# A transformer block kernel: the memory's norm and scaling moved into the linear attention's stage

## The chip, the cores and the metric

The kernel runs on one core of one Trainium2 chip. The metric is the device time of one execution in microseconds (us). In profiles PE is TensorE, DVE VectorE (Vector), ACT ScalarE (Scalar), POOL GpSimd (Pool) and SP SyncE, whose queue issues the loads.

## What is computed

Two blocks of two layers each, on a sequence of 512 tokens and 1024 features, all in float32. The change lies in both layers of the second block:

```
for i in range(2):
    hn = rmsnorm(h, ln_mix[i]);  aq, ak, av, hy, gq, gk, gv, go, glr, gates = split(hn @ w_in[i])
    y_a = attention(aq, ak, av) @ w_br_attn[i]          # branch 0
    y_b = hyena(hy) @ w_br_hyena[i]                     # branch 1
    y_c = gated_linear_attention(gq, gk, gv, go, glr) @ w_br_gla[i]   # branch 2
    h = h + (g0 * y_a + g1 * y_b + g2 * y_c) @ w_out[i]
    mn = rmsnorm(mem, ln_mem[i])                        # mem: 256 x 1024, the same in both layers
    h = h + cross_attention(rmsnorm(h, ln_x[i]), k = rmsnorm(mn @ wk), v = mn @ wv)
    h = h + square(relu(rmsnorm(h, ln_mlp[i]) @ w1)) @ w2
```

## The kernel before

Activations lie transposed in SBUF: 128 partitions of features by 512 tokens, column block by column block. Every large product is made from halves: a tensor is split into a rounded high half, which Scalar writes, and the remainder, which Vector writes (`rest`), and `mm3` sums three matmuls, high by high, high by low and low by high (lines 841 to 843). Weights come through three raw tiles (WRAW) and three split tiles (WSP): SP loads one, Scalar rounds it (line 1177), Pool subtracts (line 1518), TensorE multiplies. A projection of 1024 features takes 24 matmuls of 512 tokens, a branch's output block takes 12, and one of the memory's key projections (xk) 24 of 256 columns.

`order_of_work` writes the program as a list of steps (Unit). Where several chains run beside each other, `merged` picks the next step: the first chain in the order of its arguments whose step is due, by the times in `pe_time` and the distances in `needs`. A step that is not yet due yields to another chain. Each of the five engines' programs walks the same list and issues its own part of each step, in order. So a step that waits on one engine holds all later steps on that engine.

Each layer's `mix_second` ends with two merged stages. In the first, the linear attention (`main`: lr, gfront, gscan, gvtok, gk, gq, gexp, gmul, gturn, gstate, ginside, grun, and for each of four heads go, gout, gss, gbc, gy, split YC) is merged with the gates and output blocks of branch 0, which read the tile YAB. In the second, `memory` is merged with `last`: eight output blocks of branch 2 ("by", 12 matmuls each), the merge of the gated branches into M (products on lines 1924 and 1927, then `split` M: high half on line 1262, low half on line 1750), and the output projection (wo). The last branch's blocks take merge banks in turn:

```
return (S0, S1)[c % 2] if ab == "a" else (S0, S1, O)[c % 3]
...
b = take_pj(u) if u.pj else take(merge_bank(u.a[0], u.a[3]), dve_done, ("lo", "M", u.a[0:2], u.a[3]))
```

so a block waits until the M that used its bank has its low half. Steps with `pj` use three other banks in rotation, each free when its reader on Scalar or Vector is done.

The memory's steps are: mld (four loads into MT), msq (four squares on Scalar, line 1446, three additions on Vector, line 2159), mnorm (sum over partitions on TensorE, lines 1118 and 1119; root on Scalar, line 1449; reciprocal on Vector, line 2163), msplit (two scalings per tile on Vector, line 2170; high half on Scalar, line 1454; low half by `rest`, line 1624), then xk and xkss for four heads and eight xv. gld loads the parked gates of branch 2 (MBG). Tiles share the SBUF arena by position: MN (the split memory) lies at 8 to 15, where YAB is, and MACC and KSQ at 44 to 46, where the linear attention has QD and AM.

Of the kernel before, what the change touches and what calls it, by code (L numbers as in the profile page):

```python
# [118 lines left out]
def needs(u):  # L119

    k, a = u.kind, u.a
# [6 lines left out]
    if k == "idx":  # L128
        l, c, i = a
# [3 lines left out]
    if k == "sel":  # L133
        l, i, r = a
# [13 lines left out]
    if k == "sc":  # L148
        ab, l, c, i = a
# [42 lines left out]
    if k == "gbc":  # L192
        return [(("gss", *a), 1.8)]
    if k == "mnorm":
        return [(("msq", a[0]), 5.0)]
    if k == "msplit":
        return [(("mnorm", a[0]), 2.8 + 1.6 * a[1])]
    if k == "xkss":
        return [(("xk", *a, 1), 1.8)]
    if k == "xk":  # L200
        return [(("msplit", a[0], 3), 2.6)]
    if k == "xq":
        return [(("xsc", a[0], a[1] - 2), 0.0)]
    if k == "xqss":
# [48 lines left out]
    if k == "vturn":  # L253
        return [(("vs", a[0]), 1.2)]
    if k == "msq":
        return [(("mld", a[0]), 3.0)]
    if k == "split" and a[0] in ("YA", "YC") and a[1][0] == "a":
        return [(("cb" if a[0] == "YA" else "pmix", a[1][1], a[2]), 2.0)]
    if k == "split" and a[0] == "M" and a[1][0] == "b":
# [42 lines left out]
def order_of_work(steps):  # L302
# [100 lines left out]
    def mix_second(l):  # L403
# [58 lines left out]
        for hp in range(2):  # L462
# [8 lines left out]
            for hh in range(2):  # L471
                main += [proj("go", l, hp, hh, src=H, w=[(*B, "go", 2 * hp + hh)]), Unit("gout", l, hp, hh, o=True),
                         Unit("gss", l, hp, hh, pj=True), Unit("gbc", l, hp, hh, pj=True), Unit("gy", l, hp, hh), Unit("split", "YC", B, 2 * hp + hh)]
        out += merged(main, gated("b", l, x, 0, ("YA", B), False, False))
        last = [Unit("gld", l)]
        for c in range(8):
            last.append(proj("by", "b", l, 2, c, False, True, src=("YC", B), w=[(*B, "br", 2, c)]))
# [2 lines left out]
        last += [Unit("split", "M", B, 7)] + out_product(x, "wo", l, "b", ("M", B))  # L480
        return out + merged(memory(l), last)

    def memory(l):
        B = ("b", l)
        out = [Unit("mld", l), Unit("msq", l), Unit("mnorm", l, pj=True)] + [Unit("msplit", l, j) for j in range(4)]
        for hd in range(4):
            out += [Unit("xk", l, hd, kk, src=("MN", l), w=[(*B, "xk", 2 * hd + kk)], pj=True) for kk in range(2)]
            out += [Unit("xkss", l, hd, pj=True)]
        for half in range(2):
            out += [Unit("xv", l, half, j, src=("MN", l), w=[(*B, "xv", half, j)], t=(j == 0)) for j in range(4)]  # L490
        return out
# [77 lines left out]
def program(nc, ins, place, out, steps=8):  # L569
    ctx = ExitStack()  # L570
    with ctx:
# [40 lines left out]
        GS = at(53, "GS", 4)  # L612

        MN, MT, KM, VM = at(8, "MN", 8, fp32r), at(57, "MT", 4), at(49, "KM", 4), at(53, "VM", 4)
        MACC, KSQ = at(46, "MACC", 1), at(44, "KSQ", 2)
        YX, XQ, XSQ, XP, XPT = at(8, "YX", 16, fp32r), at(24, "XQ", 4), at(28, "XSQ", 4), at(32, "XP", 8), at(40, "XPT", 4)

        YM, XN, MR = at(0, "YM", 32, fp32r), at(32, "XN", 8), at(40, "MR", 4)

        XLS = {0: PA, 1: PA, 2: at(40, "XLB", 4), 3: at(60, "XLC", 4)}  # L620
        SQA, SQB, SQC, SQD = at(49, "SQA", 2), at(62, "SQB", 2), at(44, "SQC", 2), at(47, "SQD", 2)

        fixed("ARENA", [128, ARENA, 512])
# [542 lines left out]
        def scalar(e):  # L1166
# [32 lines left out]
            for u in plan:  # L1199
# [222 lines left out]
                elif k == "gturn":  # L1422
                    l, hp = a
                    w.wait_ge(mm_done, ("gturn", l, hp, 0))
                    e.activation(ES[:, 2 * hp, :], banks[T0][:, :], ACT.Copy).then_inc(*act_done.up(("kd", l, hp, 0)))
                elif k == "gout":
                    l, hp, hh = a
                    if hp:
                        w.wait_ge(dve_done, ("lo", "YC", ("b", l), hh))
                    w.wait_ge(mm_done, (k, *a))  # L1430
                    e.activation(GS[:, hh, :], banks[O][:, :], ACT.Square).then_inc(*act_done.up(("gsq", *a)))
                elif k == "gss":
                    l, hp, hh = a
                    w.wait_ge(mm_done, (k, *a))
                    if hp:
                        w.wait_ge(mm_done, ("gbc", l, 0, hh))
                    e.activation(SM[:, 11, 4 * hh:4 * hh + 4], pj(u)[:, 0:4], ACT.Sqrt, scale=1.0 / 128, bias=eps).then_inc(
                        *act_done.up(("pj", u.pj), (k, *a)))
                elif k == "msq":
                    l = a[0]  # L1440
                    for j in range(4):
                        w.wait_ge(landed, ("mem", l, j))
                        o = MACC[:, 0, :] if j == 0 else KSQ[:, j % 2, :]
                        if j == 3:
                            w.wait_ge(dve_done, ("macc", l, 1))
                        e.activation(o, MT[:, j, :], ACT.Square).then_inc(*act_done.up(("msq", l, j)))
                elif k == "mnorm":
                    w.wait_ge(mm_done, (k, *a))
                    e.activation(MACC[:, 0, 0:256], pj(u)[:, 0:256], ACT.Sqrt, scale=1.0 / DM, bias=eps).then_inc(
                        *act_done.up(("pj", u.pj), (k, *a)))  # L1450
                elif k == "msplit":
                    l, j = a
                    w.wait_ge(dve_done, ("mn", l, j))
                    e.activation(halves(MN, j)[0], MT[:, j, :], ACT.Copy).then_inc(*act_done.up(("mhi", l, j)))
                elif k == "xk":
                    l, hd, kk = a
                    if hd:
                        w.wait_ge(mm_done, ("xkss", l, hd - 1))
                    else:
                        w.wait_ge(dve_done, ("macc", l, 3))  # L1460
                    w.wait_ge(mm_done, (k, *a))
                    square_and_copy(u, KSQ[:, kk, 0:256], KM[:, hd, 256 * kk:256 * kk + 256], par(f"xkn{l}", kk), 256,
                                    ("xksq", *a), ("xk", *a))
                elif k == "xkss":
                    l, hd = a
                    if hd:
                        w.wait_ge(dve_done, ("xkm", l, hd - 1, 1))
                    w.wait_ge(mm_done, (k, *a))
                    e.activation(MACC[:, 0, 256:512], pj(u)[:, 0:256], ACT.Sqrt, scale=1.0 / 256, bias=eps).then_inc(
                        *act_done.up(("pj", u.pj), (k, *a)))  # L1470
                elif k == "xv" and a[2] == 3:
                    l, half, j = a
                    w.wait_ge(mm_done, (k, *a))
                    for i, b in enumerate((T0, T1)):
                        e.activation(VM[:, 2 * i + half, :], banks[b][:, :], ACT.Copy).then_inc(*act_done.up(("xvout", l, half, i)))
                elif k == "xq":
                    l, hd, kk = a
                    if hd > 1:
                        w.wait_ge(mm_done, ("xsc", l, hd - 2, 1))
                    w.wait_ge(dve_done, ("scaled", u.pj))  # L1480
                    square_and_copy(u, XSQ[:, 2 * (hd % 2) + kk, :], XQ[:, 2 * (hd % 2) + kk, :], par(f"xqn{l}", kk), 512,
                                    ("xqsq", *a), ("xq", *a))
                elif k == "xqss":
                    l, hd = a
                    w.wait_ge(mm_done, (k, *a))
                    if hd > 1:
                        w.wait_ge(act_done, ("xexp", l, hd - 2, 3))
                    e.activation(SM[:, 14 + hd % 2, 0:4], pj(u)[:, 0:4], ACT.Sqrt, scale=1.0 / 256, bias=eps).then_inc(
                        *act_done.up(("pj", u.pj), (k, *a)))
                elif k == "xsc":  # L1490
                    l, hd = a
                    m = SM[:, 6 + hd % 2, :]
                    w.wait_ge(dve_done, ("xneg", l, hd))
                    if hd > 1:
                        w.wait_ge(mm_done, ("xtr", l, hd - 2, 1))
                    for i in range(4):
                        e.activation(XP[:, 4 * (hd % 2) + i, 0:256], banks[(S0, S1)[i // 2]][:, 256 * (i % 2):256 * (i % 2) + 256],
                                     ACT.Exp, bias=m[:, 4 + i:5 + i], scale=SM[:, 14 + hd % 2, i:i + 1],
                                     accum_out=m[:, 8 + i:9 + i]).then_inc(*act_done.up(("xexp", l, hd, i)))
                elif k == "xtr":  # L1500
                    l, hd = a
                    if hd > 1:
                        w.wait_ge(mm_done, ("xpv", l, hd - 2, 1))
                    w.wait_ge(mm_done, ("xtr", l, hd, 1))
                    e.activation(XPT[:, 2 * (hd % 2) + 1, :], banks[T1][:, :], ACT.Copy).then_inc(*act_done.up(("xpt", l, hd, 1)))
# [105 lines left out]
        def vector(e):  # L1611
# [75 lines left out]
            for u in plan:  # L1687
# [472 lines left out]
                elif k == "mnorm":  # L2160
# [1 line left out]
                    w.wait_ge(act_done, (k, *a))  # L2162
                    e.reciprocal(MACC[:, 0, 0:256], MACC[:, 0, 0:256]).then_inc(*dve_done.up(("mrs", l)))
                    w.wait_ge(dve_done, ("mrs", l))
                elif k == "msplit":
                    l, j = a
                    w.wait_ge(act_done, ("msq", l, 3))
                    for kk in range(2):
                        x = MT[:, j, 256 * kk:256 * kk + 256]
                        e.scalar_tensor_tensor(x, x, par(f"lnm{l}", 2 * j + kk), MACC[:, 0, 0:256], ALU.mult, ALU.mult).then_inc(  # L2170
                            *dve_done.up(("mn0" if kk == 0 else "mn", l, j)))
                    w.wait_ge(act_done, ("mhi", l, j))
                    w.wait_ge(dve_done, ("mn", l, j))
                    rest(*halves(MN, j), MT[:, j, :], ("mlo", l, j))
# [465 lines left out]
```

## Time and profile before

| what | value |
|---|---|
| median of three runs | 3678.8 us (3678.72 to 3684.36) |
| profiled execution | 3681.5 us |
| its span in the profile | 3679.5 us |
| TensorE busy | 3482.4 us |
| Vector, Scalar, Pool busy | 1624.3, 1372.9, 1742.1 us |
| mean granted TensorE clock | 0.967 |

The span runs from the first to the last instruction in the profile. Busy time sums an engine's instructions. The granted clock is the share of full speed (2.4 GHz) that TensorE was given; 0.50 is 1.2 GHz. Matmuls overlap, so the distance between two starts, not the printed duration, is what one costs.

### The profile page before, as it was taken

The numbers are of one execution on the slowest core, as the hardware profiler recorded it, in microseconds if no ns is written. First come the engines' busy times: TensorE is split into PE (matmuls) and PEld (weight loads), VectorE is DVE, ScalarE is ACT, GpSimd is POOL, SyncE is SP. The second block draws the span as 40 slices with busy tenths as digits, with TensorE's granted clock in tenths as the row PEclk, the third lists the DMA queues.
The fourth block names the chain that finished last, engine by engine and source line by source line (L and its number), as shares of the span: only waits on it lengthen the run. The fifth ranks groups of instructions, "written<-read, shape, count | busy, mean of one in ns | idle before, by whom it ended". The sixth has DMA issues, their size and how long they took to land.

```text
span 3679.5 us, 41406 instructions
## 1 busy us (share of the span) xinstructions
PE 3482.4 (95%) x15784; PEld 2747.3 (75%) x15784; DVE 1624.3 (44%) x2605; ACT 1372.9 (37%) x2076; POOL 1742.1 (47%) x1336
## 2 busy tenths in 40 slices
PE   8999999999999987999998999999798999999999
PEld 6778787778777676668786788877675787768887
DVE  5365434366436885434432321268744434223120
ACT  3333543332543334434344322233344434443221
POOL 4454245444244774234362555657632434526564
PEclk9999999999999999989899999999899999999999
DMA  4322224223224322212351333332321214424332
GB/s 155 104 73 85 75 92 151 93 89 93 71 78 147 109 95 89 67 55 69 100 172 58 126 111 97 119 105 95 106 67 58 68 56 149 141 66 141 98 97 92
DMA packets 128846, 359.56 MB, mean 98 GB/s; under 512 B 16766, under 2 KB 17086, under 8 KB 128648
## 3 DMA queue, kind: packets, MB, share of 16 engines
q1 hardware_dynamic: 128648, 356.91, 30.1%
q8 instruction: 125, 2.05, 0.2%
q14 instruction: 73, 0.60, 0.0%
HBM read 322.24 MB, written 25.17 MB: 94 GB/s over the span
## 4 chain that ended last, share of the span: by engine, by line
PE 80%; DVE 10%; ACT 3%; issue 2%; POOL 2%; DMA 1%; SPq 1%; DVEq 0%; ACTq 0%; POOLq 0%
PE B L841 24%; PE B L843 23%; PE B L842 23%; PE B L885 2%; PE B L1003 1%; PE B L981 1%; PE B L1144 1%; SPq L2239 1%; PE B L1162 1%; DVE HY L1624 1%; PE B L1105 1%; DVE B L1621 1%; POOL WSP L1518 1%; POOL FACC L1568 1%; POOL FP L1561 1%
## 5 line engine op out<-in xcount | busy, mean ns | idle before, releaser
L1518 POOL TENSOR_TENSOR WSP<-WRAW,WSP 128x512 fp32r<-128x512 f32 x1088 | 1432.1, 1337 | 1719.1 <-ACT WSP L1177 1718.9
L841 PE MATMUL B<-H,WSP 128*128 128x512 f32 x2496 | 1011.8, 405 | 48.1 <-POOL WSP L1518 20.4
L842 PE MATMUL B<-H,WSP 128*128 128x512 f32 x2496 | 983.2, 394 | 0.0
L843 PE MATMUL B<-H,WSP 128*128 128x512 f32 x2496 | 982.6, 394 | 0.0
L1177 ACT ACTIVATE WSP<-WRAW 128x1024 fp32r<-128x1024 f32 (+1 forms) x600 | 584.2, 977 | 723.2 <-PE B L843 548.1
L841 PEld LDWEIGHTS B<-H,WSP 128*128 128x128 f32 x2496 | 475.7, 191 | 191.8 <-issue 60.4
L842 PEld LDWEIGHTS B<-H,WSP 128*128 128x128 f32 x2496 | 476.5, 191 | 101.9 <-issue 6.8
L843 PEld LDWEIGHTS B<-H,WSP 128*128 128x128 f32 x2496 | 475.2, 190 | 102.5
L1621 DVE TENSOR_TENSOR B<-B,RN 128x512 f32<-128x512 f32 x194 | 134.8, 697 | 545.8 <-PE B L843 545.7
L841 PE MATMUL B<-YM,WSP 128*128 128x512 f32 x512 | 199.5, 390 | 0.0
L843 PE MATMUL B<-YM,WSP 128*128 128x512 f32 x512 | 199.3, 389 | 0.0
L842 PE MATMUL B<-YM,WSP 128*128 128x512 f32 x512 | 199.3, 389 | 0.0
L2222 DVE SCALAR_TENSOR_TENSOR MR<-B,RN 128x512 f32<-128x512 f32 x64 | 44.1, 692 | 247.3 <-PE B L843 247.2
L2230 DVE TENSOR_TENSOR XN<-B,XN 128x512 f32<-128x512 f32 x32 | 22.1, 692 | 294.1 <-PE B L843 294.1
L1609 POOL TENSOR_TENSOR MR<-MR 128x512 f32<-128x512 f32 x64 | 88.6, 1385 | 90.8 <-DVE MR L2222 88.9
L841 PEld LDWEIGHTS B<-YM,WSP 128*128 128x128 f32 x512 | 96.1, 188 | 21.4 <-DVE XN L2230 1.6
L843 PEld LDWEIGHTS B<-YM,WSP 128*128 128x128 f32 x512 | 96.1, 188 | 20.0
L842 PEld LDWEIGHTS B<-YM,WSP 128*128 128x128 f32 x512 | 96.1, 188 | 19.9
L1187 ACT ACTIVATE GA<-B 128x512 f32<-128x512 f32 x48 | 28.7, 599 | 208.4 <-DVE B L1621 208.4
L841 PE MATMUL B<-YAC,WSP 128*128 128x512 f32 x256 | 102.7, 401 | 0.0
L843 PE MATMUL B<-YAC,WSP 128*128 128x512 f32 x256 | 99.9, 390 | 0.0
L842 PE MATMUL B<-YAC,WSP 128*128 128x512 f32 x256 | 99.7, 390 | 0.0
(422 smaller groups left out, 5409.1 us busy)
## 6 DMA issues: line engine op xcount, KB each, us to landing
WRAW<-in_wb SPq DMA_DIRECT2D x318, 512.0 KB, 3.6
WRAW<-in_wa SPq DMA_DIRECT2D x154, 512.0 KB, 3.6
WRAW<-in_wa SPq DMA_DIRECT2D x48, 256.0 KB, 2.6
WRAW<-in_wb SPq DMA_DIRECT2D x48, 256.0 KB, 2.7
WRAW<-in_wd SPq DMA_DIRECT2D x16, 512.0 KB, 3.8
QA<-RXA SPq DMA_DIRECT2D x64, 64.0 KB, 2.0
PA<-xs SPq DMA_DIRECT2D x16, 256.0 KB, 2.7
xs<-PA SPq DMA_DIRECT2D x16, 256.0 KB, 4.4
```

Of the source, the lines that this page charges most:

```text
L841: e.matmul(o, L[0], R[0], start=first, stop=False)
L842: e.matmul(o, L[0], R[1], start=False, stop=False)
L843: return e.matmul(o, L[1], R[0], start=False, stop=last)
L885: x = e.transpose(b[:, 128 * i:128 * i + 128], src[i], eye)
L981: e.matmul(b[:, 0:n], q, kk, start=True, stop=True).then_inc(*mm_done.up(("sc", ab, l, c, i, hh)))
L1003: x = e.matmul(b[64 * hh:64 * hh + 64, q0:512], v, PT[:, 4 * hh + j, q0:512], start=j == 0, stop=j == 3)
L1105: x = e.matmul(b[:, 64 * n:64 * n + 64], SS[half, 2 * d + n // 4, 128 * (n % 4):128 * (n % 4) + 128], QD[half, d, 64 * n:64 * n + 64], sta ...
L1177: e.activation(WSP[:, i % NSP, 0, 0:n * cols], WRAW[:, i % NRAW, 0:n * cols], ACT.Copy).then_inc(*hi_done.up(i))
L1518: x = e.tensor_tensor(WSP[:, i % NSP, 1, c:c + CUT], WRAW[:, i % NRAW, c:c + CUT], WSP[:, i % NSP, 0, c:c + CUT].bitcast(fp32), ALU.subtract)
L1609: e.tensor_tensor(t, t, t, ALU.mult).then_inc(*pool_done.up((k, *a)))
L1621: e.tensor_tensor(pj(u)[:, :], pj(u)[:, :], RN[:, :], ALU.mult).then_inc(*dve_done.up(("scaled", u.pj)))
L2222: e.scalar_tensor_tensor(MR[:, c % 4, :], pj(u)[:, :], 0.0, RN[:, :], ALU.max, ALU.mult).then_inc(*dve_done.up(("pj", u.pj), (k, *a)))
```

## The change

The step list `memory` is cut in two. Its front (mld, msq, mnorm and the four scalings, now a step of their own, mscale) becomes a chain merged into the linear attention's stage, second in order between `main` and branch 0's blocks. The rounding (msplit) stays in the last branch's stage, each of its four steps due behind one of that branch's blocks, and Scalar's part waits for the last block that reads YAB. msq is due behind the linear attention's last `ginside`. MACC and KSQ move to 40 to 42, where GKQ and KI are dead by then; the residual's ring XLB moves from 40 to 43.

```diff
@@ needs
     if k == "mnorm":
-        return [(("msq", a[0]), 5.0)]
+        return [(("msq", a[0]), 2.0)]
     if k == "msplit":
-        return [(("mnorm", a[0]), 2.8 + 1.6 * a[1])]
+        return [(("by", "b", a[0], 2, a[1], False, True), 0.0)]
+    if k == "mscale":
+        return [(("mnorm", a[0]), 2.8 + 1.2 * a[1])]
     if k == "xk":
-        return [(("msplit", a[0], 3), 2.6)]
+        return [(("msplit", a[0], 3), 5.0)]
     if k == "msq":
-        return [(("mld", a[0]), 3.0)]
+        return [(("mld", a[0]), 3.0), (("ginside", a[0], 1, 1), 1.0)]
@@ mix_second
-        out += merged(main, gated("b", l, x, 0, ("YA", B), False, False))
+        out += merged(main, memory_front(l), gated("b", l, x, 0, ("YA", B), False, False))
+    def memory_front(l):
+        return [Unit("mld", l), Unit("msq", l), Unit("mnorm", l, pj=True)] + [Unit("mscale", l, j) for j in range(4)]
+
     def memory(l):
         B = ("b", l)
-        out = [Unit("mld", l), Unit("msq", l), Unit("mnorm", l, pj=True)] + [Unit("msplit", l, j) for j in range(4)]
+        out = [Unit("msplit", l, j) for j in range(4)]
@@ program
-        MACC, KSQ = at(46, "MACC", 1), at(44, "KSQ", 2)
+        MACC, KSQ = at(40, "MACC", 1), at(41, "KSQ", 2)
-        XLS = {0: PA, 1: PA, 2: at(40, "XLB", 4), 3: at(60, "XLC", 4)}
+        XLS = {0: PA, 1: PA, 2: at(43, "XLB", 4), 3: at(60, "XLC", 4)}
@@ scalar
                 elif k == "msq":
                     l = a[0]
+                    w.wait_ge(dve_done, ("gmul", l, 1, 1))
+                    w.wait_ge(mm_done, ("ginside", l, 1, 1, 1))
                 elif k == "msplit":
                     l, j = a
+                    w.wait_ge(mm_done, ("by", "b", l, 0, 7, False, False))
                     w.wait_ge(dve_done, ("mn", l, j))
@@ vector
-                elif k == "msplit":
+                elif k == "mscale":
                     l, j = a
                     w.wait_ge(act_done, ("msq", l, 3))
                     for kk in range(2):
...
+                elif k == "msplit":
+                    l, j = a
                     w.wait_ge(act_done, ("mhi", l, j))
                     w.wait_ge(dve_done, ("mn", l, j))
                     rest(*halves(MN, j), MT[:, j, :], ("mlo", l, j))
```

## Rows read from the trace of the kernel before

**Rows 1.** The page's head and busy times, all engines.

```profile
span 3679.5 us, 41406 instructions
...
PE 3482.4 (95%) x15784; PEld 2747.3 (75%) x15784; DVE 1624.3 (44%) x2605; ACT 1372.9 (37%) x2076; POOL 1742.1 (47%) x1336
```

**Rows 2.** Waits of TensorE, whole span: us in total, times, longest.

```profile
PE B L841 <- DVE MB L1750: 9.9, 5, 2.7
```

**Rows 3.** Timeline of TensorE, layer 0's last branch: start, us, engine, line, idle before.

```profile
1806.42 0.59 PE L1118 MATMUL B<-MACC,CST 128*128 128x256 f32 x2
...
1807.10 0.58 PE L841 MATMUL B<-YBC,WSP 128*128 128x512 f32 x1
...
1812.82 0.79 PE L841 MATMUL B<-YBC,WSP 128*128 128x512 f32 x1 [2.60 <-DVE MB L1750]
...
1819.16 0.52 PE L841 MATMUL B<-YBC,WSP 128*128 128x512 f32 x1 [1.80 <-DVE MB L1750]
...
1823.61 0.40 PE L841 MATMUL B<-YBC,WSP 128*128 128x512 f32 x1
...
1826.36 0.28 PE L841 MATMUL B<-MN,WSP 128*128 128x256 f32 x1
```

**Rows 4.** Windows: length, busy us of each engine (x instructions), granted clock, DMA.

```profile
1807.10:1810.00 2.90, 2.90 (x14) 2.23 (x12) 2.83 (x4) 0.47 (x1) 0.87 (x1) 1.00 0.53 154
1812.80:1816.00 3.20, 3.18 (x8) 2.50 (x9) 2.47 (x5) 0.63 (x1) 0.99 (x1) 0.50 0.37 100
```

**Rows 5.** Timeline of Vector and Scalar, layer 0's last branch.

```profile
1804.60 0.70 DVE L1927 TENSOR_TENSOR B<-B,MSB 128x512 f32<-128x512 f32 x1
...
1808.06 1.74 DVE L2163 RECIPROCAL MACC<-MACC 128x256 f32<-128x256 f32 x1
...
1809.84 0.88 DVE L2170 SCALAR_TENSOR_TENSOR MT<-MT,PAR,MACC 128x256 f32<-128x256 f32 x2
...
1811.35 0.58 ACT L1262 ACTIVATE MB<-B 128x512 fp32r<-128x512 f32 x1
...
1812.08 0.68 DVE L1750 SCALAR_TENSOR_TENSOR MB<-B,MB 128x512 fp32r<-128x512 f32 x1
```

**Rows 6.** Timeline of TensorE, layer 1's last branch.

```profile
3061.06 0.59 PE L1118 MATMUL B<-MACC,CST 128*128 128x256 f32 x2
...
3068.31 0.50 PE L841 MATMUL B<-YBC,WSP 128*128 128x512 f32 x1 [2.72 <-DVE MB L1750]
...
3081.61 0.31 PE L841 MATMUL B<-MN,WSP 128*128 128x256 f32 x1
```

**Rows 7.** Groups by line, Vector, 1797.15 to 1826.36: busy, mean ns, idle before.

```profile
L1927 DVE TENSOR_TENSOR B<-B,MSB 128x512 f32<-128x512 f32 x6 | 4.2, 700 | 0.2
...
L2170 DVE SCALAR_TENSOR_TENSOR MT<-MT,PAR,MACC 128x256 f32<-128x256 f32 x8 | 3.5, 478 | 0.0
L1750 DVE SCALAR_TENSOR_TENSOR MB<-B,MB 128x512 fp32r<-128x512 f32 x5 | 3.4, 685 | 0.6 <-ACT MB L1262 0.6
L1624 DVE TENSOR_TENSOR MN<-MT,MN 128x512 fp32r<-128x512 f32 x4 | 2.8, 692 | 2.9 <-ACT MN L1454 2.9
```

**Rows 8.** One tile's instructions (KSQ): ns min/median/max, first and last start.

```profile
L1446 ACT ACTIVATE KSQ<-MT x6: 614/617/633, 1799.4 to 3054.8; 128x512 f32<-128x512 f32 x6
```

**Rows 9.** Timeline of TensorE and Vector around the sum of squares of head 2.

```profile
1769.87 0.47 PE L841 MATMUL B<-H,WSP 128*128 128x512 f32 x1
...
1770.45 0.69 DVE L1929 TENSOR_TENSOR MSB<-B,MSB 128x512 f32<-128x512 f32 x1
```

**Rows 10.** Timeline of TensorE, Scalar and SP, the linear attention's start and end.

```profile
1603.95 1.95 PE L1063 MATMUL B<-LR,WL 32*128 32x512 f32 x4 [1.41 <-DVE RST L2059]
...
1616.26 1.99 ACT L1177 ACTIVATE WSP<-WRAW 128x1024 fp32r<-128x1024 f32 x2
...
1793.21 1.75 SPq L2239 DMA_DIRECT2D MT<-in_mem  x4
```

**Rows 11.** One tile's instructions (HY) on Vector: ns min/median/max, first and last start.

```profile
L1624 DVE TENSOR_TENSOR HY<-TS,HY x8: 1767/1774/1784, 1328.7 to 2641.4; 128x512 fp32r<-128x512 f32 x8
```

## The prediction

> **What bounds the kernel now.** The page says it first: TensorE is busy for 3482 us of a span of 3679.5 us [rows 1]. An operation elsewhere counts only if TensorE waits for it or if TensorE's own work changes. So the second view is the table of waits of TensorE over the span. One line of it belongs to the place of this change: before a block of matmuls TensorE waits for Vector's instruction on line 1750, the low half of the merged tile M, five times, 9.9 us in all [rows 2]. The third view, the timeline, says where. In layer 0 the fourth block of the last branch has run when TensorE stops until 1812.82, and again until 1819.16 [rows 3]. Layer 1 does the same from 3068.31 on [rows 6].
>
> These waits cost more than their length. In a stretch of the block ahead of the first stop the granted clock is 1.00 (2.4 GHz); in the stretch behind it, 0.50 (1.2 GHz), with 8 matmuls recorded in 3.2 us against 14 in 2.9 us [rows 4].
>
> Why is M's low half late? The last branch has three merge banks, so block c can start only when M of block c-3 has been written out of its bank. M of column block 1 is complete when the product on line 1927 ends, at 1804.60 + 0.70 = 1805.30. Its low half starts at 1812.08. Between them Vector is in the memory's reciprocal (1.74 us), its first two scalings (0.88 us), and the wait for Scalar's rounding. Scalar's high half of M, queued behind the same rounding, starts at 1811.35 [rows 5]. The memory's norm and scaling stand in front of M in two queues.
>
> **The change part by part.** (1) *Taken out of the last branch:* four squares on Scalar of 0.617 us [rows 8], three additions of the products' shape (0.70 us) and the reciprocal on Vector, eight scalings of 0.478 us [rows 5, 7], and on TensorE the norm's four matmuls, 1807.10 - 1806.42 = 0.68 us [rows 3]. What stays per column block on Vector is 0.70 twice for the products, 0.69 for the memory's low half and 0.69 for M's low half [rows 7]: about 2.8 us. One block of twelve matmuls takes 1826.36 - 1823.61 = 2.75 us at full clock [rows 3]. The two are almost equal, so the long waits should go and short ones stay.
>
> Walked through for layer 0: block 1's products end at 1805.30, the second memory rounding at 1806.0, M 0's low half at 1806.7, while TensorE is free at 1806.42, the old start of the norm. That is a wait of about 0.4 us. Block 2's products end near 1808.1 (TensorE done 1806.6, two products of 0.70); the third rounding and M 1's low half end at 1809.5, about when block 4 needs it. Block 5 wants M 2 and waits another 0.4 us. Waits that short are assumed to leave the clock up. In the new order the key projections (xk) wait for the fourth rounding plus a planned 5 us, so they come after six blocks instead of seven; I count the seventh in both. The seven blocks are then done at 1806.42 + 4 x 2.75 + 0.8 = 1818.2 instead of 1826.36: 8.1 us. For layer 1 the same sum is 3061.06 + 11.8 = 3072.9 instead of 3081.61: 8.7 us [rows 3, 6]. Together 16.9 us, in which the norm's matmuls are included as gone.
>
> (2) *Put into the linear attention.* By the planner's due times I place the squares behind the output of head 2 (hp 1, hh 0), the norm on TensorE behind that head's sum of squares (gss), two scalings behind it and two behind the last head's output. The norm's matmuls cost their 0.68 us here. They also shift the rotation of the three projection banks by one: the gate block that follows now takes the bank of branch 0's block 6, which Vector frees at 1770.45 + 0.69 = 1771.14. TensorE would start that gate at 1769.87 + 0.68 = 1770.55 [rows 9], so it waits about 0.6 us. Price: 1.3 us a layer, 2.6 us in all. I take layer 0's price for both.
>
> The squares begin when Scalar has squared the head's output, just behind the end of branch 0's previous work. Four squares, one wait and two additions behind them are some 4 us, and TensorE has 2.75 us or more of block 6 plus the sum of squares to do before the norm. I cost this at nothing: the cover is block 6. Without it TensorE would wait those 4 us. Behind the squares in Scalar's queue stands a weight rounding for the projection after the gate, which is a full gate block away. Vector has its room for the reciprocal (1.74 us) and the scalings (2 x 0.88 us) under that gate block and under the last head's output. I cost them at nothing too. If the reciprocal and two scalings were all in the way of the next product, that would be 3.5 us a layer.
>
> (3) *The loads.* Four issues on SP, 1.75 us, and in front of them a wait for branch 0's last block [rows 10]. They move to the start of the stage, behind a wait for the small projection lr. That projection is over before 1603.95, and behind the four issues stands the weight load whose rounding Scalar reaches at 1616.26 [rows 10], a dozen us later; I cost it at nothing. At the old place the eight gate loads and the weight loads of the last branch are no longer behind that wait, and the 1.75 us of issues ahead of them are gone too: they come sooner by at least that. That is part of why the walk above has no wait for weights.
>
> (4) *The rounding's new wait* (for the last reader of YAB) is met before Scalar gets there, because branch 0 is over. The other moved tiles (norm scratch, the residual's ring) add no wait that I find.
>
> (5) *Contention.* The kernel's subtractions with two SBUF tensors sometimes take far longer than 0.69 us: those that read TS take 1.77 us in the middle, while the memory's low halves took 0.692 us on average [rows 7, 11]. Pool was mostly idle beside them. In the new order a weight's subtraction on Pool starts just before several of the roundings. From below this costs nothing. From above it costs 1.77 - 0.69 = 1.08 us for each of the three roundings whose lateness reaches a bank, 3.2 us a layer. Walking Pool's queue beside Vector's, two of the three are met, each for about half of Pool's instruction, and part of that falls into Vector's slack. I take 0.9 us a layer, 1.8 us in all.
>
> The Trainium skill (SBUF — State Buffer, section "SBUF: two separate sides") says that a Vector operation with two SBUF inputs and a GpSimd operation that reads SBUF share a pair of ports, held exclusively for a whole instruction. The trace's 1.77 us against 0.69 us agrees in kind. By it every meeting would count in full, and the sum would go towards the upper price; by the 0.69 us rows alone it would be nothing.
>
> **Sum.** 16.9 - 2.6 - 1.8 = 12.5 us. The profiled execution took 3681.5 us (its span is 3679.5 us), so it would become 3669.0 us. The median of the runs is 3678.8 us, 2.7 us under it, and the same difference gives **3666.3 us**.
>
> **The rivals.** *A, as above.* Its own range is 3663 to 3670 us: without contention 3664.5, with neither contention nor short waits nearly 3663, with contention at twice my price 3668.
>
> *B, the rounding takes over the wait.* Pool meets all the roundings, M is again late by more than a us a block, and the clock falls again. Price: 3 x 1.08 for the roundings and 1.6 us for eight matmuls at half clock [rows 4], 4.9 us a layer. The gain of 14.3 us without contention shrinks to 4.5 us: 3674 us. For it speaks Vector's 2.8 us against 2.75 us, which leaves no room. Against it: Pool needs one short subtraction per block here.
>
> *C, no measurable difference.* What is won is given back behind the last branch: the key and value projections take a weight of double size for 24 short matmuls each, and started closer together they may wait for Pool or the loads. To cancel the gain they must lose 6 us a layer. Against it: the supply is started by TensorE's progress and not by a clock of its own. About 3677 us.
>
> *D, slower.* The memory's load holds SP at the start of the stage and the weight behind it lands late. It decides if that weight lands later than 1616.26; beyond that each us is paid on TensorE in both layers, plus 1.6 us each for the clock. To end at 3685 us it would have to land some 8 us late. Against it: a dozen us of room for 1.75 us of issues and their landing.
>
> **How the numbers follow.** A 0.78, B 0.10, C 0.08, D 0.04. Changes of under 0.2% (7.4 us) can't be told from none here. A and a tenth of B lie beyond that: faster 0.79. The rest of B, and C, are within it: 0.17. Slower 0.04. The range runs from 3662 us (A with every short wait gone, and a little of the slow start of the branch as well) to 3673 us (most of the way to B), which leaves out C, D and half of B.
>
> **What would show it.** In the profile after: the waits for line 1750 down from 9.9 us to under 3 us; granted clock 1.00 through blocks 3 to 5; the norm's matmuls right behind a sum of squares in the linear attention, and a wait of about 0.6 us behind them for line 1929; low halves of the memory between 0.69 and 1.8 us; the MT loads near the start of the stage with no new wait for line 1518. The prediction is wrong if the sum of waits for M stays above 5 us, if the planner puts the norm where TensorE waits for the additions, or if new waits for weights stand among the key projections.

## The result and the profile after

The changed kernel takes 3659.5 us (median of four runs, 3657.5 to 3662.5) against 3678.8 us before (four runs, 3675.2 to 3684.4): a ratio of 0.9947, interval 0.993 to 0.9964. It is faster, as forecast, by 19.2 us where 12.5 were forecast, and 3659.5 us lies below the forecast range of 3662 to 3673 us. The profiled execution took 3659.6 us. The page's head and busy times after:

```profile
span 3657.7 us, 41410 instructions
...
PE 3463.9 (95%) x15784; PEld 2731.9 (75%) x15784; DVE 1622.5 (44%) x2605; ACT 1374.2 (38%) x2076; POOL 1742.3 (48%) x1336
```

TensorE has the same number of instructions as before and is busy 18.5 us less [rows 1]; the span fell by 21.8 us. Most of the time came from matmuls that run faster, not from shorter waits. The table of TensorE's waits, after:

```profile
PE B L846 <- DVE MB L1758: 3.3, 4, 1.0
...
PE B L846 <- DVE YBC L1632: 1.0, 2, 0.7
```

The wait for M's low half (line 1758 now, 1750 in [rows 2]) is down from 9.9 us to 3.3 us and no single one is longer than 1.03 us. A short wait for the last head's low half (YBC) stands at the start of the branch, 0.34 and 0.70 us; the kernel before, whose clock falls at the last head, does not have it. Windows of layer 0's stage after: from the first matmul that reads LR to the last head's output block; that output block (`gout`); branch 0's block 7; up to the first block of branch 2; up to the first key projection; up to the next stage's first product. The columns are those of [rows 4].

```profile
1600.86:1779.37 178.51, 174.34 (x941) 142.67 (x941) 74.19 (x119) 74.31 (x102) 77.21 (x57) 0.97 0.21 72
1779.37:1784.62 5.25, 5.25 (x38) 4.50 (x36) 2.27 (x5) 0.60 (x1) 0.00 (x0) 1.00 0.00 0
1784.62:1787.47 2.85, 2.85 (x14) 2.35 (x13) 0.00 (x0) 2.40 (x3) 1.28 (x1) 1.00 0.54 178
1787.47:1790.88 3.41, 1.86 (x18) 1.78 (x16) 2.13 (x4) 0.26 (x1) 0.00 (x0) 1.00 0.92 302
1790.88:1810.24 19.36, 17.37 (x75) 13.33 (x74) 15.10 (x20) 9.65 (x15) 10.63 (x8) 1.00 0.47 161
1810.24:1909.02 98.78, 97.56 (x521) 84.51 (x520) 35.48 (x40) 45.07 (x68) 65.22 (x51) 1.00 0.50 172
```

The same windows before (there the stretch behind branch 2's first block ends with the seventh block, not the sixth):

```profile
1603.95:1781.81 177.86, 175.09 (x937) 143.48 (x938) 68.68 (x111) 71.76 (x97) 77.23 (x57) 0.96 0.20 61
1781.81:1788.37 6.56, 6.56 (x37) 5.61 (x35) 0.70 (x1) 0.60 (x1) 0.00 (x0) 0.77 0.00 0
1788.37:1793.01 4.64, 4.64 (x13) 3.69 (x13) 0.00 (x0) 2.40 (x3) 1.27 (x1) 0.59 0.00 0
1793.01:1797.15 4.14, 2.59 (x17) 2.50 (x16) 2.13 (x4) 0.26 (x1) 0.00 (x0) 0.82 0.72 219
1797.15:1826.36 29.21, 24.80 (x90) 19.33 (x90) 22.29 (x35) 12.96 (x22) 9.48 (x8) 0.85 0.46 158
1826.36:1922.44 96.08, 94.86 (x509) 82.28 (x508) 34.76 (x37) 43.95 (x66) 65.91 (x51) 1.00 0.55 178
```

The last two rows of each table are the place that the prediction looked at: 29.21 + 96.08 = 125.29 us before, 19.36 + 98.78 = 118.14 us after, 7.15 us less, now at clock 1.00. Some 2.4 us of it is idle time, 0.7 us the norm's matmuls, and the rest, some 4 us, matmuls at the higher clock. The three rows above them are a surprise. Before, TensorE had half clock in part of the last head's output block and most of block 7 behind it (0.77 and 0.59, with no idle time in either); after, it has 1.00 in both. That gives 1.31 + 1.79 + 0.73 = 3.83 us. The first row grew by 0.65 us. So the whole stage went from 318.49 to 308.16 us in layer 0. In layer 1 it went from 322.08 to 308.65 us, 7.98 us of it in the last branch. Outside the two stages the traces differ by 2.0 us the other way (3.1 less ahead, 4.4 more between the layers, 0.7 more behind): -10.33 - 13.43 + 2.0 = -21.8 us, the whole change of the span. The 4.4 us are chance: second traces of the two kernels have 937.8 and 937.5 us between the layers, as the changed kernel here (937.6), and only this trace of the kernel before has 933.2. The 3.1 us are within what executions differ by: ahead of the first stage, where all the kernels of this case have the same steps, their traces vary between 1598.7 and 1606.3 us.

Layer 0 in detail. Timeline of TensorE where the norm now stands, and in the last branch:

```profile
1765.74 0.95 PE L1118 MATMUL B<-CST,GS 128*128 128x1 f32 x8
1766.54 0.68 PE L1123 MATMUL B<-MACC,CST 128*128 128x256 f32 x2
1767.06 0.59 PE L1124 MATMUL B<-MACC,CST 128*128 128x256 f32 x2
1767.41 0.50 PE L846 MATMUL B<-H,WSP 128*128 128x512 f32 x1
...
1800.59 0.50 PE L846 MATMUL B<-YBC,WSP 128*128 128x512 f32 x1 [0.61 <-DVE MB L1758]
...
1807.37 0.50 PE L846 MATMUL B<-YBC,WSP 128*128 128x512 f32 x1 [1.03 <-DVE MB L1758]
1810.24 0.28 PE L846 MATMUL B<-MN,WSP 128*128 128x256 f32 x1
```

Timeline of Vector: the instruction that frees the gate block's bank, then the memory's four low halves; and Pool beside them:

```profile
1766.66 0.69 DVE L1937 TENSOR_TENSOR MSB<-B,MSB 128x512 f32<-128x512 f32 x1
...
1795.95 1.22 DVE L1632 TENSOR_TENSOR MN<-MT,MN 128x512 fp32r<-128x512 f32 x1
1798.74 1.19 DVE L1632 TENSOR_TENSOR MN<-MT,MN 128x512 fp32r<-128x512 f32 x1
...
1801.78 0.87 DVE L1632 TENSOR_TENSOR MN<-MT,MN 128x512 fp32r<-128x512 f32 x1
...
1805.09 1.63 DVE L1632 TENSOR_TENSOR MN<-MT,MN 128x512 fp32r<-128x512 f32 x1
```

```profile
1795.32 1.29 POOL L1526 TENSOR_TENSOR WSP<-WRAW,WSP 128x512 fp32r<-128x512 f32 x1 [0.72 <-ACT WSP L1182]
1798.08 1.30 POOL L1526 TENSOR_TENSOR WSP<-WRAW,WSP 128x512 fp32r<-128x512 f32 x1 [1.47 <-ACT WSP L1182]
1800.80 1.30 POOL L1526 TENSOR_TENSOR WSP<-WRAW,WSP 128x512 fp32r<-128x512 f32 x1 [1.42 <-ACT WSP L1182]
1804.87 4.25 POOL L1526 TENSOR_TENSOR WSP<-WRAW,WSP 128x512 fp32r<-128x512 f32 x3 [2.77 <-ACT WSP L1182]
```

All four low halves meet Pool and take 1.22, 1.19, 0.87 and 1.63 us, 4.91 us in place of 4 x 0.69 = 2.76 [rows 7]. The first three end 0.56, 0.55 and 0.55 us after Pool's instruction does (1795.95 + 1.22 against 1795.32 + 1.29, and so on); the fourth ends 0.43 us after the first of the three in its row (4.25 / 3 = 1.42 us each).

### The profile page after: what moved, and what is told of

It is laid out like the page before. It is cut to its first block, busy times and chain, and to the rows that moved or that the text cites. A ratio compares the mean times of both kernels' runs of the same rounds, so it can differ in the third digit from the quotient of the medians.

```text
span 3657.7 us, 41410 instructions
## 1 busy us (share of the span) xinstructions
PE 3463.9 (95%) x15784; PEld 2731.9 (75%) x15784; DVE 1622.5 (44%) x2605; ACT 1374.2 (38%) x2076; POOL 1742.3 (48%) x1336
## 4 chain that ended last, share of the span: by engine, by line
PE 80%; DVE 10%; ACT 3%; issue 3%; POOL 2%; DMA 1%; SPq 1%; DVEq 0%; ACTq 0%; POOLq 0%
PE B L846 24%; PE B L848 23%; PE B L847 23%; PE B L890 2%; PE B L1008 1%; PE B L986 1%; POOL WSP L1526 1%; PE B L1167 1%; DVE HY L1632 1%; PE B L1149 1%; SPq L2249 1%; DVE B L1629 1%; PE B L1110 1%; POOL FACC L1576 1%; POOL FP L1569 1%
```

## The experiments

The question after the result was the clock at the last head, which no term of the sum had. The norm's step delays TensorE by 1767.41 - 1766.54 = 0.87 us ahead of the gate block, some 12 us before the last head. Theory: it is this shift in time that lets the clock hold. Rivals: the last branch's new order or the moved loads, the norm's matmuls as work, or chance from run to run. Ratios below are against runs of the kernel before on the same chip.

**Both kernels again** (one profiled execution each, unchanged).

> The kernel before once more, for a second profile. Theory 'place': the granted clock falls in the last head's output and the branch 0 block behind it in both layers again (the block of twelve near 4.6 us instead of 2.9), since the program puts TensorE's thin work there at the same distances. Rival 'chance': where the clock falls differs from one execution to the next, and in at least one of the two layers that block takes 2.9 us.

> The changed kernel once more. Theory 'place': clock at 1.00 from the last head's output to the end of the last branch in both layers, the block of twelve 2.9 us. Rival 'chance': in at least one layer the clock falls there and the block takes about 4.6 us. Both: waits for the merge near 0.6 and 1.0 us a layer, as they hang on Vector's queue.

3683.8 and 3664.4 us. In the kernel before, the last head's output block took 6.54 and 6.66 us in the two layers; in the changed one 5.24 us twice. It is a property of the kernels. The second trace of the kernel before also shows that layer 1's 322.08 us was not typical: it is 318.47 us here, with 125.41 us in the last branch, so that the changed kernel's 118.56 us there are 6.85 us less and not 7.98. The changed kernel can lose such a stretch too: its layer 1 had a slow second head (6.88 us, elsewhere 5.25) in this execution, and its stage took 311.68 us.

**The delay alone, in the kernel before.** Two matmuls of 128x256, overwritten afterwards, ahead of the third head's sum of squares.

```diff
                     w.wait_ge(act_done, ("gsq", *a))
+                    if hp == 1 and hh == 0:
+                        for i in range(2):
+                            e.matmul(b[:, 0:256], ones, GS[:, 0, 256 * i:256 * i + 256], start=True, stop=True)
```

> The kernel before with two matmuls more on TensorE behind the third head's output, some 0.9 us, whose result is overwritten; nothing else is changed. Theory 'place': 0.9 us of denser work at that spot shifts what follows and the clock stays up at the last head's output: two layers at -5 us each, +0.9 us each, so near 3671 us. Rival 'chance': no help, +1.8 us, 3680 us.

3674.8 us, ratio 0.9982 (0.9972 to 0.9991): added work makes the kernel faster, by 6.7 us with an interval of 3 to 10. The windows of the last head and block 7, both layers:

```profile
1779.30:1784.55 5.25, 5.25 (x38) 4.49 (x36) 0.70 (x1) 0.60 (x1) 0.00 (x0) 1.00 0.00 0
1784.55:1787.40 2.85, 2.85 (x13) 2.36 (x13) 0.00 (x0) 2.40 (x3) 1.28 (x1) 1.00 0.00 0
3031.93:3037.17 5.24, 5.24 (x37) 4.49 (x35) 0.70 (x1) 0.60 (x1) 0.00 (x0) 1.00 0.00 0
3037.17:3040.03 2.86, 2.86 (x14) 2.37 (x14) 0.00 (x0) 2.40 (x3) 1.28 (x1) 1.00 0.03 6
```

The last branch keeps its old waits (line 1753 here, 11.9 us), and takes 1.1 and 2.0 us longer than in the second trace of the kernel before (126.60 and 127.36 us against 125.51 and 125.41). So the two stages give only 3.1 us of the difference between these traces (316.53 + 317.31 against 318.50 + 318.47 us); what the medians show beyond that is not explained by the last head. So the clock at the last head needs neither the new order nor the moved loads.

**The loads alone** (mld moved, the rest as before).

```diff
-        out += merged(main, gated("b", l, x, 0, ("YA", B), False, False))
+        out += merged(main, [Unit("mld", l)], gated("b", l, x, 0, ("YA", B), False, False))
...
-        out = [Unit("mld", l), Unit("msq", l), Unit("mnorm", l, pj=True)] + [Unit("msplit", l, j) for j in range(4)]
+        out = [Unit("msq", l), Unit("mnorm", l, pj=True)] + [Unit("msplit", l, j) for j in range(4)]
```

> The kernel before with the memory's four loads alone moved to the start of the linear attention's stage. Theory: the loads were hidden and stay hidden, within 1 us of before. Rival: gate loads and weights 1.75 us and more sooner shorten the last branch by up to 2 us a layer; or the loads hold SP at the stage's start and TensorE waits for a weight there (over 1.7 us before block two of gvtok).

3679.5 us, 0.9992 (0.9983 to 1.0001): no difference. The stages take 318.05 and 317.94 us, the last head 6.60 and 6.61 us.

**The norm moved, the scalings left in the last branch.** The changed kernel, with each mscale put directly ahead of its msplit in the last branch.

```diff
     if k == "mscale":
-        return [(("mnorm", a[0]), 2.8 + 1.2 * a[1])]
+        return [(("by", "b", a[0], 2, a[1], False, True), 0.0)]
...
-        return [Unit("mld", l), Unit("msq", l), Unit("mnorm", l, pj=True)] + [Unit("mscale", l, j) for j in range(4)]
+        return [Unit("mld", l), Unit("msq", l), Unit("mnorm", l, pj=True)]
...
-        out = [Unit("msplit", l, j) for j in range(4)]
+        out = [v for j in range(4) for v in (Unit("mscale", l, j), Unit("msplit", l, j))]
```

> The change with the scalings left in the last branch, each right ahead of its rounding; load, squares and norm moved as in the change. Vector's work per block rises from 2.8 to 3.7 us against TensorE's 2.75, so blocks 3 to 5 each wait about 1 us more: waits for the merge near 4 to 5 us a layer instead of 1.7, about 3665 us if the clock holds. Rival: the scalings were the main brake, and the waits return to 5 us a layer with the half clock, 3672 us.

3670.8 us (3664.4 to 3671.6), 0.9968 (0.9955 to 0.9981). The trace is of the fastest of the five runs; the other four took 3669.5 to 3671.6 us. TensorE's waits and two of Vector's rows:

```profile
PE B L846 <- DVE MB L1758: 8.5, 4, 2.5
```

```profile
1797.33 0.87 DVE L2178 SCALAR_TENSOR_TENSOR MT<-MT,PAR,MACC 128x256 f32<-128x256 f32 x2
1798.95 0.69 DVE L1632 TENSOR_TENSOR MN<-MT,MN 128x512 fp32r<-128x512 f32 x1 [0.75 <-ACT MN L1462]
```

Vector now idles 0.75 us in each column block while Scalar rounds what Vector has just scaled. From branch 2's first block to the next product it takes 122.41 us in layer 0, 4.3 us more than in the changed kernel (3.7 us in layer 1) and only 2.9 us less than before. Moving the scalings is the larger part of the gain here. The waits came as the theory had them (4.3 us a layer), the median nearer to the rival's 3672 us than to its 3665. The low halves take 0.69 us in this order, and the last head has full clock.

**The norm's matmuls left out of the changed kernel.** The bank and the order stay; the root is taken of sums that were not added over the partitions, so the memory's norm is not the reference's.

```diff
                     w.wait_ge(dve_done, ("macc", a[0], 3))
-                    e.matmul(b[:, 0:256], ones, MACC[:, 0, 0:256], start=True, stop=False)
-                    e.matmul(b[:, 0:256], ones, MACC[:, 0, 256:512], start=False, stop=True).then_inc(*mm_done.up((k, *a)))
...
-                    w.wait_ge(mm_done, (k, *a))
+                    w.wait_ge(dve_done, ("macc", a[0], 3))
...
```

> The change without the norm's four matmuls (the root is taken of each partition's own sum, so the memory is wrongly normalized); all other steps and queues the same. Theory 'place': without these 0.9 us the last head's output falls to half clock in both layers as in the kernel before, by 3.9 us a layer; -1.7 us of matmuls, +7.8 us: about 3666 us, and the block behind the last head at 4.6 us. Rival 'other': the clock holds for another cause (loads, Vector, Scalar), and it is 1.7 us faster than the change, 3658 us.

3663.0 us, 0.995 (0.9935 to 0.9965), with full clock at both last heads. The expected fall did not come, for a reason that the timeline gives:

```profile
1767.96 0.95 PE L1118 MATMUL B<-CST,GS 128*128 128x1 f32 x8
1769.64 0.50 PE L846 MATMUL B<-H,WSP 128*128 128x512 f32 x1 [0.73 <-DVE MSB L1934]
```

The gate block starts 1.68 us behind the start of the sum of squares, as with the matmuls (1767.41 - 1765.74 = 1.67 us). The wait for the bank is there anyway; in the changed kernel the matmuls fill it. This run takes the work away and keeps the delay, and the clock holds.

**No delay either.** The same, and the norm takes no bank, so that the gate block's bank is the old one.

```diff
-        return [Unit("mld", l), Unit("msq", l), Unit("mnorm", l, pj=True)] + [Unit("mscale", l, j) for j in range(4)]
+        return [Unit("mld", l), Unit("msq", l), Unit("mnorm", l)] + [Unit("mscale", l, j) for j in range(4)]
```

> The run without the norm's matmuls again, and now the norm takes no projection bank either, so TensorE has neither the matmuls nor the wait of 0.7 us for the bank in its place (the memory is again wrongly normalized). Theory 'shift': with no delay behind the third head's sum of squares the last head's output falls to half clock again in both layers as in the kernel before (block behind it 4.6 us): +3.9 and -0.9 us a layer against the change, about 3666 us. Rival: the clock holds here for another reason than the delay; then it is 0.9 us a layer faster than the change, about 3658 us.

3665.9 us, 0.9955 (0.994 to 0.997). Its interval overlaps that of the changed kernel, so the times alone do not decide, but the spans are 3664.1 and 3657.7 us, and the windows of the last head and block 7 show where:

```profile
1778.21:1784.79 6.58, 6.58 (x38) 5.62 (x36) 2.27 (x5) 0.60 (x1) 0.00 (x0) 0.77 0.00 0
1784.79:1789.42 4.63, 4.63 (x14) 3.67 (x14) 0.00 (x0) 2.40 (x3) 1.27 (x1) 0.59 0.73 214
3027.40:3033.90 6.50, 6.50 (x37) 5.54 (x35) 2.27 (x5) 0.60 (x1) 0.00 (x0) 0.78 0.00 0
3033.90:3038.60 4.70, 4.70 (x14) 3.70 (x14) 0.00 (x0) 2.40 (x3) 1.27 (x1) 0.58 0.71 231
```

The clock falls again in both layers, although Vector, Scalar and the loads have their new work. The stages take 311.32 and 311.51 us, 3.0 us a layer above the changed kernel's; the last branch keeps its gain (118.35 and 118.57 us).

**Other delays, in the kernel before.** One and four of the filler matmuls in place of two; and no filler, but a wait of the gate block for the sum of branch 0's block 6, so that TensorE idles.

```diff
+                if u.kind == "gate" and u.a[0] == "b" and u.a[2:] == (0, 7):
+                    w.wait_ge(dve_done, ("by", "b", u.a[1], 0, 6))
```

> The kernel before with one matmul more (some 0.4 us) instead of two behind the third head's sum of squares. Theory 'shift' with a narrow margin: half the delay is not always enough, the clock falls in one or both layers; between 3675 and 3682 us. If any small shift does it: both layers hold, 3674 us.

> The kernel before with four such matmuls (some 1.7 us) in the same place. Theory 'shift': what counts is the distance from the third head's output to the last one's, so a longer shift can bring the fall back; if it does not, the clock holds in both layers and the time is 1.7 us above the run with two, about 3676 us. If it comes back: 3684 us.

> The kernel before with one wait: the gate block behind the third head's sum of squares waits for Vector's sum into MSB of branch 0's block 6, some 1.3 us in which TensorE stands idle, a little more than the 0.9 us of matmuls in the fill run. If a shift in time is what counts, the clock stays up at the last head's output as it did there: 3674 us or less. If the activity itself counts, idle time does not help: the block behind the last head stays at 4.6 us and the time is 3684 us.

One: 3677.7 us, 0.9985 (0.9972 to 0.9997), spread from 3665.2 to 3685.7 (the kernel before on that chip: 3672.8 to 3691.7). Four: 3677.7 us, 0.9993 (0.9983 to 1.0003). Idle: 3679.9 us, 0.9994 (0.9985 to 1.0003), between its two expected times. With four, the clock fell too, in layer 0 only behind the output block:

```profile
1779.65:1784.89 5.24, 5.24 (x37) 4.49 (x35) 0.70 (x1) 0.60 (x1) 0.00 (x0) 1.00 0.00 0
1784.89:1789.33 4.44, 4.44 (x14) 3.57 (x14) 0.00 (x0) 2.40 (x3) 1.28 (x1) 0.62 0.00 0
```

In layer 0 of the idle run the clock fell a further time, inside the gate block that had waited (clock 0.76), so the last head came 13.53 us behind the gate's start in place of 11.94, and some 2.9 us late in all:

```profile
1769.35:1776.52 7.17, 7.17 (x25) 5.75 (x26) 0.69 (x2) 0.92 (x1) 0.98 (x1) 0.76 0.12 37
```

All traces side by side. Delay is the distance from the start of the third head's sum of squares (with fillers, from the first of them) to the gate block, less the 0.81 us of the kernel before; the last two columns are the last head's output block and block 7, us, in layer 0 and layer 1.

| kernels | delay, us | made of | output block | block 7 |
|---|---|---|---|---|
| before, again, loads alone | 0 | | 6.5 to 6.7 (once 5.68) | 4.5 to 5.3 |
| changed without delay | 0 | | 6.58, 6.50 | 4.63, 4.70 |
| one filler | 0.43 | matmuls | 6.90, 5.24 | 4.31, 2.86 |
| two fillers | 0.86 | matmuls | 5.25, 5.24 | 2.85, 2.86 |
| changed, again, norm moved alone, M first (below) | 0.86 | norm | 5.24 or 5.25 | 2.85 or 2.86 |
| changed without the norm's matmuls | 0.86 | idle | 5.25, 5.24 | 2.85, 2.86 |
| idle in the kernel before | 1.3 (2.9 at the last head), 1.0 | idle | 6.22, 5.25 | 4.98, 2.85 |
| four fillers | 1.73 | matmuls | 5.24, 5.62 | 4.44, 5.29 |

Where nothing was added the clock fell in all eight layers traced, at 0.86 us in none of twelve, and between and beyond it went either way. Work or idleness made no difference at 0.86 us. So the moment decides, and the gain is not the norm's own. Beyond 0.86 us the evidence is thin, since the history ahead also counts. In most layers the output blocks of the second and third head take 5.24 or 5.25 us and some 6.5 us. With four fillers they took 6.04 and 5.40 us in layer 1, so the clock had fallen at other places before the delay. That leaves layer 0 with four fillers as the one plain case of a longer delay that loses the clock. (Layer 1 of the first trace before was unusual in the same way, with 6.22 and 5.62 us; it is the 5.68 of the table, and half clock stretched its distance to the gate block by 0.34 us.)

**M's rounding ahead of the memory's.** A version that came out of this: each msplit waits in the plan for the split of the M before it, so Vector's and Scalar's order alone changes.

```diff
-        return [(("by", "b", a[0], 2, a[1], False, True), 0.0)]
+        return [(("by", "b", a[0], 2, a[1], False, True), 0.0)] + ([(("split", "M", ("b", a[0]), a[1] - 1), 0.0)] if a[1] else [])
```

> The change with one more distance for the planner: each rounding of the memory is due behind the split of M of the column block before. TensorE's order is the same; Vector and Scalar write M's halves ahead of the memory's. Theory: the 1.6 us a layer that blocks 3 and 5 still wait for M come from the roundings ahead of it on Vector, lengthened by Pool, so they vanish and the time falls by about 3 us against the change, to 3657 us (0.9938 of before). Rival: the matmul of M's bank waits for the products, not the rounding; the waits stay at 0.6 and 1.0 us, 3660 us.

3653.7 us (3652.9 to 3658.9), 0.9927 (0.9914 to 0.9939): better than the kernel before, as is clear from the times. The interval touches that of the changed kernel (0.993 to 0.9964), so against it the stages of the traces have to decide. TensorE has no wait for M left. The memory's low halves on Vector:

```profile
1795.88 1.21 DVE L1632 TENSOR_TENSOR MN<-MT,MN 128x512 fp32r<-128x512 f32 x1
...
1799.27 0.68 DVE L1632 TENSOR_TENSOR MN<-MT,MN 128x512 fp32r<-128x512 f32 x1
...
1801.98 0.68 DVE L1632 TENSOR_TENSOR MN<-MT,MN 128x512 fp32r<-128x512 f32 x1
...
1804.70 1.03 DVE L1632 TENSOR_TENSOR MN<-MT,MN 128x512 fp32r<-128x512 f32 x1
```

They sum to 3.60 us in place of 4.91, and what is left of the contention falls behind M's rounding, where no bank waits for it. The stages take 305.85 and 306.28 us, 2.3 us less a layer.

## Why the prediction was wrong, and where it was right

The direction and the last branch came out as forecast. The time fell below the range because of one term of the sum, the price of the move into the linear attention.

*The last branch, terms (1) and (5): right in mechanism and size.* With the 0.9 us of contention taken off, the walk gave 8.1 - 0.9 = 7.2 us in layer 0 and 7.8 in layer 1; measured were 7.15 and 7.98 (6.85 against the second trace of the kernel before). The key projections come after six blocks, as planned. The two waits in layer 0 are 0.61 and 1.03 us, where 0.4 and 0.4 were forecast without contention: 0.84 us more, the price of 0.9. The composition differs: all four roundings were lengthened, not two, by 2.15 us together, and slack took 1.3 us of it; that 0.84 came so close to 0.9 is partly luck. The waits for M sum to 3.3 us, a little over the 3 us that were named. Clock 1.00 held through blocks 3 to 5. The Trainium skill (SBUF — State Buffer, section "SBUF: two separate sides") has such operations of Vector and GpSimd exclude each other for whole instructions. The rows agree in kind: at each of the four meetings in the changed kernel's layer 0 Vector ended 0.43 to 0.56 us behind Pool's instruction, whether 0.32 or 1.2 us of that were left; what came behind is less than the 0.69 us that Vector takes alone.

*The move into the linear attention, term (2): this is the step that failed.* It was priced at +1.3 us a layer. The place was right (squares behind head 2, the norm behind its sum of squares, no wait for the additions, everything on Scalar and Vector hidden), but two things were not. The norm's matmuls and the bank's wait were added, 0.68 + 0.6; they lie in parallel. Vector frees the bank at 1766.66 + 0.69 = 1767.35 and the norm ends by 1767.41, so the price is 0.87 us. That is the small error. The large one: the profile of before had 6.56 and 4.64 us for the last head's output block and block 7, part of them at half clock, and the sum took them as given: what the shift would do to them stood at nothing. A shift of 0.87 us gave back 2.9 to 3.2 us a layer net of itself (the run without the delay). Term (2) is thus -3.2 us in layer 0 (and about -3.0 in layer 1 by the more typical trace) in place of +1.3: with it the forecast of 12.5 us becomes 12.5 + 2 x (1.3 + 3.1) = 21.3 us, against 19.2 measured between the medians and 21.8 between the traces. The changed kernel without the delay gained 15.2 us on its chip (3665.9 against 3681.1); less 2 x 0.87 us for the delay itself that is an estimated 13.5 us, close to the 12.5 of the prediction, which had the delay and the slow last head.

*The loads, the new wait, terms (3) and (4): nothing, as forecast.* The loads alone make no difference. TensorE's wait for Pool at the start of the stage is 1.7 us after and 1.6 before.

*The rivals.* B would have kept M late by more than 1 us a block and the clock low; the waits are 3.3 us over both layers and the clock is 1.00. C would have given the gain back behind the branch; from the first key projection on there is no new wait, and the 98.78 us hold one block more than the 96.08 before. D is refuted by the loads alone. The run with the scalings left in place is near B: there Vector's scalings and its wait for Scalar keep M late, and some 4 us a layer are lost.

What stays open: what the throttle looks at. The runs show that the outcome depends on when the last head's block starts, not why 0.86 us held in every trace and 1.73 us did not. The third head's output block keeps its slow clock in the version with M's rounding first too (some 6.5 us in both layers, against 5.24 at full clock), and no run tried to win it back. Nor do the runs tell whether the gain at the last head would survive another edit ahead of it.

## What to carry to other kernels

Where a profile has stretches at half clock with no idle time, they are a term of any change ahead of them: ask for the windows of granted clock over the whole stage, and widen the range by what they hold, since a shift of under 1 us can win or lose it. A step moved beside a wait that it causes itself costs the longer of the two, not their sum. When two engines' work per column block is as long as TensorE's, put first in each queue what frees a bank; the rest can be late.

## What the runs showed of the hardware

TensorE's granted clock fell inside a block of small float32 matmuls (128x128 and 64x64) without idle time (the last head's output block: mean 0.77, 6.56 us instead of 5.25) and was still low in part of the full-size matmuls behind it (0.59, 4.64 us instead of 2.85). These are its two levels mixed; idle time is not needed for a fall. Whether it fell changed with a delay of 0.86 us some 12 us earlier, and two useless matmuls in that place made the kernel 6.7 us faster (3674.8 against 3681.5 us on the same chip), 3.1 us of it in the two stages of the traces. In one trace the gate block behind a wait of 1.21 us was partly at half clock (0.76). The shift's share of run-to-run spread is not shown: one filler spread over 20.5 us and two over 5.2 us, but on chips where the kernel before spread over 18.8 and 8.7 us.
